# x and memory laid out by features in a one-core block kernel: loads, queues and fourteen transposes changed

## What is computed

```python
def _rmsnorm(x, g, eps=NORM_EPS):
    xf = x.astype(jnp.float32)
    y = xf * lax.rsqrt(jnp.mean(xf * xf, axis=-1, keepdims=True) + eps)
    return (y * g.astype(jnp.float32)).astype(x.dtype)
...
    x = x + 0.5 * _rmsnorm(_swiglu(_rmsnorm(x, ffn1_pre_g), ffn1_w_gu, ffn1_w_down), ffn1_post_g)
...
    kx, vx = jnp.split(_rmsnorm(mem, mem_norm_g) @ xa_w_kv, 2, axis=-1)
```

## Time and profile before

| what | value |
|---|---|
| median of 3 runs | 1097.92 us |
| the profiled execution | 1097.21 us |
| its span | 1095.4 us |
| PE busy | 1083.8 us, 99% |
| DVE busy | 797.0 us, 73% |
| ACT busy | 593.2 us, 54% |
| HBM read | 186.50 MB, 171 GB/s over the span |

### The profile page before, as it was taken

The page is one execution under the profiler, slowest core; times in us unless marked ns, Lnnn a source line. Parts: engine busy times, 40 slices in busy tenths (PEclk is TensorE's granted clock), DMA queues, the critical chain, the costliest instruction groups (busy, mean ns, idle before and its releaser), DMA issues.

```text
span 1095.4 us, 21019 instructions
## 1 busy us (share of the span) xinstructions
PE 1083.8 (99%) x8538; PEld 1029.7 (94%) x8538; DVE 797.0 (73%) x1119; ACT 593.2 (54%) x845; POOL 0.2 (0%) x4
## 2 busy tenths in 40 slices
PE   9999999999999999999999999999999998999998
PEld 7999999999999999999999988999999798999998
DVE  6665556989989867778778556765555887997774
ACT  5544445678643345878446546444444665565561
POOL 0000000000000000000000000000000000000000
PEclk9999999999999999999999999999999999999999
DMA  8765555455533354443556533465555346443341
GB/s 301 249 228 191 195 188 192 158 197 185 171 138 116 121 206 155 154 172 137 205 169 236 192 116 116 148 227 191 197 186 191 127 167 223 159 154 123 109 154 39
DMA packets 29137, 188.59 MB, mean 172 GB/s; under 512 B 3496, under 2 KB 4809, under 8 KB 7370
## 3 DMA queue, kind: packets, MB, share of 16 engines
q1 hardware_dynamic: 26592, 181.42, 47.7%
q10 hardware_dynamic: 2474, 6.15, 1.7%
HBM read 186.50 MB, written 1.05 MB: 171 GB/s over the span
## 4 chain that ended last, share of the span: by engine, by line
PE 91%; DVE 5%; ACT 2%; issue 1%; DMA 1%; SPq 0%; DVEq 0%; ACTq 0%
PE bank L520 16%; PE bank L521 16%; PE bank L522 16%; PE bank L532 11%; PE bank L533 11%; PE bank L534 11%; PE bank L619 3%; DVE sb_w_lo L2043 1%; PE bank L745 1%; PE bank L860 1%; ACT sb_w_hi L1346 1%; PE bank L1008 1%; PE bank L693 1%; PE bank L1020 1%; DMA sb_w_raw<-in_w 1%
## 5 line engine op out<-in xcount | busy, mean ns | idle before, releaser
L2043 DVE TENSOR_TENSOR sb_w_lo<-sb_w_raw,sb_w_hi 128x2048 fp32r<-128x2048 f32 x169 | 386.5, 2289 | 135.6 <-ACT sb_w_hi L1346 135.2
L1346 ACT ACTIVATE sb_w_hi<-sb_w_raw 128x2048 fp32r<-128x2048 f32 x169 | 322.9, 1911 | 34.5 <-PE bank L522 33.0
L520 PE MATMUL bank<-sb_hT_hi,sb_w_hi 128*128 128x256 f32 (+1 forms) x816 | 226.0, 277 | 0.0
L522 PE MATMUL bank<-sb_hT_hi,sb_w_lo 128*128 128x256 f32 (+1 forms) x816 | 226.0, 277 | 0.0
L521 PE MATMUL bank<-sb_hT_lo,sb_w_hi 128*128 128x256 f32 (+1 forms) x816 | 225.8, 277 | 0.0
L532 PE MATMUL bank<-sb_hT_hi,sb_w_hi 128*128 128x256 f32 (+2 forms) x744 | 212.7, 286 | 0.0
L533 PE MATMUL bank<-sb_hT_lo,sb_w_hi 128*128 128x256 f32 (+2 forms) x744 | 206.4, 277 | 0.0
L534 PE MATMUL bank<-sb_hT_hi,sb_w_lo 128*128 128x256 f32 x744 | 206.2, 277 | 0.0
L522 PEld LDWEIGHTS bank<-sb_hT_hi,sb_w_lo 128*128 128x128 f32 (+1 forms) x816 | 152.8, 187 | 0.1
L520 PEld LDWEIGHTS bank<-sb_hT_hi,sb_w_hi 128*128 128x128 f32 (+1 forms) x816 | 152.8, 187 | 0.0
L521 PEld LDWEIGHTS bank<-sb_hT_lo,sb_w_hi 128*128 128x128 f32 (+1 forms) x816 | 152.5, 187 | 0.0
(11 more groups left out here) (507 smaller groups left out, 2137.9 us busy)
## 6 DMA issues: line engine op xcount, KB each, us to landing
sb_w_raw<-in_w SPq DMA_DIRECT2D x169, 1024.0 KB, 5.0
sb_x<-in_x SPq DMA_DIRECT2D x2, 512.0 KB, 4.5
sb_w_raw<-in_w SPq DMA_DIRECT2D x4, 256.0 KB, 6.8
sb_w_raw<-in_w SPq DMA_DIRECT2D x2, 512.0 KB, 8.0
sb_mem_xn<-in_mem ACTq DMA_DIRECT2D x1, 1024.0 KB, 7.8
sb_post_g<-in_ffn_post_g ACTq DMA_DIRECT2D x2, 512.0 KB, 4.6
sb_decay<-in_c_decay ACTq DMA_DIRECT2D x1, 768.0 KB, 4.2
out<-sb_x SPq DMA_DIRECT2D x3, 256.0 KB, 2.1
```

Of the source, the lines that this page charges most:

```text
L520: pe.matmul(o, a_hi, b_hi, start=first, stop=False)
L522: return pe.matmul(o, a_lo, b_hi, start=False, stop=last)
L1346: act.activation(w_hi[b % STAGES][:], w_raw[b % RING][:], ACT.Copy).then_inc(w_hi_in, 1)
L2043: tt(w_lo[b % STAGES][:], w_raw[b % RING][:], f32(w_hi[b % STAGES][:]), ALU.subtract).then_inc(w_lo_in, 1)
```

## The change

`x` and `mem` are also handed over transposed (`xT`, `memT`). SP loads `xT` in four parts of 256 KB straight into `hT`, alternating with the four parts of block 0, and only behind block 2 the rows of `x`, the identity and `cols`. ACT's queue first loads the 8 gain columns (`first_g`); ACT and DVE multiply the even and odd feature tiles of `hT` by them in place. The transposes of `x` go. PE does one product of zeros, one that opens bank 0, and then block 0 feature tile by feature tile. The squares of `x` are both summed on ACT, behind the rounding of block 2; the root follows the remainder of block 2 on DVE; PE spreads it in the middle of up 2 (not up 1). The remainder of block 3 is written before hidden tile 0 (not behind it), and ACT rounds block 3 before it copies `rb`. Of `mem`, the root alone is spread by two transposes, in front of up 20; DVE multiplies `mem_T` by gain and root in eight pieces, ACT and DVE split it in two halves. One DVE operation of 128x2048 behind kv (`mem_T` from hi and lo, L2324) goes.

```diff
             def first_block():
-                ready = norm_done(0)
                 o = claim("up1.0", 0, 0)
+                pe.matmul(o[:], zeros[:, 0:P], zeros[:], start=True, stop=False)
                 w = w_raw[0][:].rearrange("p (k c) -> p k c", k=KD)
-                for i in range(2):
-                    for k in range(KD):
...
+                for k in range(KD):
+                    pe.wait_ge(S("x_odd" if k % 2 else "x_even"), k // 2 + 1)
...
+                    for i in range(2):
...
-                    up_block(j, between=(lambda: root_turn(n)) if j == 1 else None)
+                    up_block(j, between=(lambda: root_turn(n)) if j == 3 - n else None)
...
+                if n == 1:
+                    mem_root_turn()
                 up_block(FF_TILES - 2)
                 down_block(PAIRS - 2, 0, *LAST_DOWN[n][2])
                 up_block(FF_TILES - 1)
-
-                if n == 1:
-                    norm_turn(1, mem_xn, 1, (7, 0, 2, 1))
                 down_block(PAIRS - 1)
...
-            stay_warm(zeros[:, 0:P], zeros[:], 2)
-
-            pe.wait_ge(S("ident_in"), 16)
-            raw_turn(0, x_landed)
+            stay_warm(zeros[:, 0:P], zeros[:], 1)
...
@@ scalar
+                if n == 1:
+                    after(up_at(n, 0))
                 o = full(act, f"rb{n}")
                 copy(f"rb{n}", f["rb"][:], o[:, 0:SEQ])
                 gate(0)
...
                     act.dma_start(mem_xn[:], a["mem"].rearrange("(t p) d -> p t d", p=P)).then_inc(S("mem_in"), 16)
+                    act.dma_start(mem_T[:].rearrange("p k c -> p (k c)"), a["memT"]).then_inc(S("memT_in"), 16)
...
                 after(down_at(n, PAIRS - 2))
+                if n == 1:
+                    mem_high(0)
                 gate(FF_TILES - 1)
                 high(FF_TILES - 1)
                 after(up_at(n, FF_TILES - 1))
                 if n == 1:
-                    norm_high(1, "mem_norm_g", mem_hi)
+                    mem_high(1)
...
+            act.dma_start(first_g[:], a["cols"][:, at:at + KD]).then_inc(S("first_g_in"), 16)
+            act.wait_ge(S("zeros"), 1)
+            act.activation(ffn[1]["gate"][:, 0, :], zeros[:, 0:SEQ], ACT.Silu)
...
             round_to(STAGES)
+            for t in range(TOK):
+                act.wait_ge(S(f"x_in{t}"), 16)
+                ins = act.activation(ffn[1]["xn"][:, t, :], x[:, t, :], ACT.Square, accum_out=ssq[:, t:t + 1])
+            ins.then_inc(S("norm_ssq"), 1)
+            act.wait_ge(S("cols_in"), 16)
...
@@ vector
+                if n == 1:
+                    low_block(b)
                 wait_read(dve, f"rb{n}")
                 if n == 1:
-                    hidden_tile(0, [], [b])
+                    hidden_tile(0, [], [])
                     hidden_tile(1, [], [b + 1])
...
                     row_root(1, rstd[:, 0:2])
+                    dve.tensor_copy(mem_r[:], rstd[:, 0:2]).then_inc(S("mem_root"), 1)
...
+                    mem_normal(0, 2)
+                    hidden_tile(FF_TILES - 2, [b], [b + 1], 0, [lambda: mem_normal(2, 5), lambda: mem_normal(5, 8)])
+                    hidden_tile(FF_TILES - 1, [], [b + 2], 0, [lambda: mem_low(0)])
+                    mem_low(1)
...
+            low_to(STAGES)
             ffn_root(0)
-            low_to(STAGES)
...
@@ sync
-            for t in range(TOK):
-                sp.dma_start(x[:, t, :], a["x"][t * P:(t + 1) * P, :]).then_inc(S(f"x_in{t}"), 16)
+            n = KD // FIRST_PARTS
             for b, parts in ((0, FIRST_PARTS), (1, SECOND_PARTS), (2, 1)):
                 for part in range(parts):
+                    if b == 0:
+                        sp.dma_start(hT[:, part * n:(part + 1) * n, :].rearrange("p k c -> p (k c)"),
+                                     a["xT"][:, part * n * SEQ:(part + 1) * n * SEQ]).then_inc(S(f"xT_in{part}"), 16)
...
+            for t in range(TOK):
+                sp.dma_start(x[:, t, :], a["x"][t * P:(t + 1) * P, :]).then_inc(S(f"x_in{t}"), 16)
+            sp.dma_start(ident, a["c_square"][:, 0:P]).then_inc(S("ident_in"), 16)
+            sp.dma_start(cols[:], a["cols"]).then_inc(S("cols_in"), 16)
```

More of the change, by code:

```diff
@@ L184 @@
 SPLIT_FROM = 1
-RAW = (0, 3, 4, 5)
+RAW = (3, 4, 5)
 def columns_of(n):
     return ((0,), (1, 2), (3, 4), (5, 6), (7,)) if n in RAW else ((0, 1), (2, 3), (4, 5), (6, 7))
-COLUMNS_AT = [sum(len(columns_of(m)) for m in range(1, n)) for n in range(7)]
-BY_SCALAR, BY_VECTOR = (0, 2, 4), (1, 3)
+COLUMNS_AT = [sum(len(columns_of(m)) for m in range(2, n)) for n in range(7)]
 FOLD_AT = (0, 1, 1 + P)
@@ L338, in program @@
         mem_T = place(8, "mem_T", [P, KD, SEQ])
+        mem_r = place(80, "mem_r", [P, TOK])
+        mem_rb = place(98, "mem_rb", [P, SEQ])
         late_hi = place(32, "late_hi", [P, KD, SEQ], F32R)
@@ L1443, in ffn_part, with mem_high @@
                 rounded[0] += TURN * PAIR_TURNS
+                if n == 1:
+                    o = full(act, "mem_rb")
+                    copy("mem_rb", mem_rb[:], o[:, 0:SEQ])
+                def mem_high(side):
+                    act.wait_ge(S("mem_n"), 4 * side + 4)
+                    k = slice(4 * side, 4 * side + 4)
+                    act.activation(mem_hi[:, k, :], mem_T[:, k, :], ACT.Copy).then_inc(S("mem_hi"), 1)
                 gate(FF_TILES - 2)
@@ L1484, in out_part @@
                 after(FIRST[stage] + 3)
[L1487 to L1502, removed]
+            at = COLS["ffn1_pre_g"][0]
+            act.dma_start(first_g[:], a["cols"][:, at:at + KD]).then_inc(S("first_g_in"), 16)
+            act.wait_ge(S("zeros"), 1)
+            act.activation(ffn[1]["gate"][:, 0, :], zeros[:, 0:SEQ], ACT.Silu)
+            act.wait_ge(S("first_g_in"), 16)
+            for k in range(0, KD, 2):
+                act.wait_ge(S(f"xT_in{k // (KD // FIRST_PARTS)}"), 16)
+                act.activation(hT[:, k, :], hT[:, k, :], ACT.Copy, scale=first_g[:, k:k + 1]).then_inc(S("x_even"), 1)
+            for side in range(2):
+                act.wait_ge(S("x_even"), 2 * side + 2)
+                act.wait_ge(S("x_odd"), 2 * side + 2)
                 k = slice(4 * side, 4 * side + 4)
@@ L2219, in ffn_part, with mem_normal, mem_low @@
                 if n == 1:
[L2220 to L2223, removed]
+                    def mem_normal(first, last):
+                        for k in range(first, last):
+                            stt(mem_T[:, k, :], mem_T[:, k, :], col("mem_norm_g", k), mem_rb[:], ALU.mult, ALU.mult)\
+                                .then_inc(S("mem_n"), 1)
+                    def mem_low(side):
+                        dve.wait_ge(S("mem_hi"), side + 1)
+                        k = slice(4 * side, 4 * side + 4)
+                        tt(mem_lo[:, k, :], mem_T[:, k, :], f32(mem_hi[:, k, :]), ALU.subtract).then_inc(S("mem_lo"), 1)
+                    dve.wait_ge(S("memT_in"), 16)
+                    dve.wait_ge(S("cols_in"), 16)
+                    wait_read(dve, "mem_rb")
+                    mem_normal(0, 2)
+                    hidden_tile(FF_TILES - 2, [b], [b + 1], 0, [lambda: mem_normal(2, 5), lambda: mem_normal(5, 8)])
+                    hidden_tile(FF_TILES - 1, [], [b + 2], 0, [lambda: mem_low(0)])
+                    mem_low(1)
                 else:
@@ L2299, in _ @@
             dve.memset(zeros[:], 0.0).then_inc(S("zeros"), 1)
[L2300 to L2307, removed]
+            dve.wait_ge(S("first_g_in"), 16)
+            for k in range(1, KD, 2):
+                dve.wait_ge(S(f"xT_in{k // (KD // FIRST_PARTS)}"), 16)
+                ts(hT[:, k, :], hT[:, k, :], first_g[:, k:k + 1], None, ALU.mult).then_inc(S("x_odd"), 1)
             for side in range(2):
@@ L2992 @@
     arrays = {"x": given["x"][0], "mem": given["mem"][0]}
+    for n in ("x", "mem"):
+        arrays[n + "T"] = arrays[n].T.reshape(KD, P, SEQ).transpose(1, 0, 2).reshape(P, KD * SEQ)
     stream = np.zeros((NBLOCK, P, BLOCK), np.float32)
```

41 lines of the change are left out of this document (22 added, 19 removed).

## The result

The changed kernel takes 1104.52 us (median of 5 runs, 1102.80 to 1108.13), the kernel before 1096.92 us beside it (5 runs, 1095.55 to 1098.52): a ratio of 1.0069 with a 95% interval of 1.0046 to 1.0092. The change makes the kernel **7.6 us slower**. Forecast were 1097.4 and "same"; the range ended at 1100.0.

A forecast was written before the change was run, and what follows sets the result against it. PE, busy 99% of the span, was taken to bound the kernel. Start +1.20 and end of the first feed-forward part -1.66 gave -0.5 us: 1097.4 against the median of 1097.92, range 1094.6 to 1100.0.

The forecast's parts named there:

- The start (+1.20): Kernel start to up 6: up 1 begins 1.6 us earlier, but block 3 is rounded later; PE starts up 6 1.20 us later.
- The last link: Up 6: block 8's remainder comes 1.56 us later with 0.36 to spare, so PE starts up 6 1.20 us later.
- the rule that I had set against the sum: Loads of xT: transfers of 1 MiB or more advised for 75% of peak; quarters take 3.3 us, total 0.8 us later.
- The end of the first feed-forward part (-1.66): Before kv0: mem's transposes go, kv0 waits 0.4 us for the second half of mem_lo; 1.66 us gained.
- The sum -0.5: Whole kernel: +1.20 at the start and -1.66 at the end of the first feed-forward part give -0.5 us.
- Rivals 1, 2 and 4: 1: early start kept, 1094.6 (0.14). 2: block 3 lands late, 1100.5 (0.11). 4: mem splitting on DVE replaces transposes, 1099.1 (0.12).
- Rival 3 (0.03): Start: PE waits on first pieces, loses its 2.4 GHz clock, block 0 takes 14.3 us; +2.9 us, 1100.8; chance 0.03.

The follow-up runs named there:

- both parts: The changed kernel with first_g placed behind the placed tiles, so these stand as before the change: 1096.56 us, ratio 0.9990.
- memory alone: The kernel before with only the changed path of memory, start as before: 1095.48 us, ratio 0.9985.
- the last run: The changed kernel with first_g behind the placed tiles, and identity and cols loaded behind block 3 instead of ahead: 1097.40 us, ratio 0.9995.

## Why the prediction was wrong

**Right, in the main.** The start (+1.20): the profile of the changed kernel shows +1.23 at up 6, of which 0.22 are the slower products of down 0 and down 1, so the start costs 1.0 there. Block 3, the remainder, the tiles and down 0 follow each other as worked out, and moving 0.2 MB behind block 3 moves block 3 and down 0 together. The last link was wrong: PE didn't wait for block 8's remainder at up 6, it brought most of its delay from down 0 (+0.73, forecast +0.3) and up 3 (+1.01, forecast +0.65). That 1.23 stands so close to 1.20 is luck. In the totals it costs 2.0 (1.0 to 3.0) by itself, or 1.1 as the difference of both parts (1096.56) and memory alone (1095.48). Up 1 came at 14.04, not 13.3: block 1's first half was rounded from 11.58 and not from 10.93. It did no harm, as down 0 waits for tile 0 anyway. By the rule that I had set against the sum (the Trainium skill, DMA: Bandwidth & Descriptors, section Bandwidth) it would have come 0.8 us later than by mine, and it came 0.65 later. (The 0.8 took the rule's 75% of the peak for the quarters as well; the rule gives that share from 1 MiB up, so by it 0.8 is the least.) The stretch from 5 to 10 us moved 333 GB/s, the next 413. But the kernel before, whose x comes in bigger loads, moved 323 in the same stretch, so the trace doesn't show that the size of the pieces is the reason. The end of the first feed-forward part (-1.66): -1.6 by the trace. The sum -0.5: with the tiles back in place the full change measures -1.3 by the medians, -1.1 by the ratio (0.9990, 0.9981 to 0.9999), inside my range. Rivals 1, 2 and 4 didn't come. Rival 3 (0.03) came in part in two profiles of the changed start, for 1.0 us: I had the right mechanism, a wait on the pieces and before up 1, and took the 0.80 us gap of the earlier trace rows as a reason against it, but PE waits some 2 us before up 1. (That the zeros run at the 1.2 GHz level was read from their 0.88 us a record; the granted clock that the profile gives for that stretch is 1.00.)

**The step that failed** is one that isn't in the working. The change part by part went through the removed and the added instructions, and took every other PE step as before: behind up 6 "PE is the slower of the three and nothing more is lost", and "The 128x2048 sum of mem_T on DVE goes behind kv, beside PE's work: nothing" is its last word on the rest of the kernel. The runs show 0.9 us lost between up 6 and kv0 with PE busy throughout, and most of the rest behind it. The diff line `first_g = sb("first_g", [P, KD])` isn't costed in any sentence. It moves every placed tile by 32 bytes, and that costs 8.0 us (1104.52 against 1096.56; 7.8 by itself in the kernel before), sixteen times the sum that I had worked out. Neither a rival nor the range had anything of the kind, since every cost in them hung on a wait, a transfer or a clock. The kernel before holds a hint: it places the ffn tiles at `24 + LINE` (in KB, LINE being 64 / 1024), 64 bytes off the grid of the others, and the prediction doesn't ask what such an offset is worth.

**Open.** Why the products with hT and the weights, none of which moved, also lose 2.2 us with 32 bytes, outside the feed-forward parts, and with 64 bytes inside them too. As they read no placed tile, what the other engines do at the time with the placed tiles may have a part in it; that isn't shown. Their step goes between 113 and 118 ns from stage to stage in the kernel before too. And which two accesses get in each other's way: the runs show that the distance counts, not what is done with it inside the chip. A run that moves the weights alone wasn't made.

## What to carry to other kernels

A new tile changes the addresses of all tiles allocated behind it. When PE is 99% busy, put a small tile last, or pad it to a distance that costs nothing in your own runs (in these, 256 and 512 bytes), and compare the step of products in a stage that the change doesn't touch: if it differs, the time has moved for a reason outside the change. Run an unused tile of the same size in the old kernel as a control before a change is blamed or dropped. Here the shift hid a part worth some 1.6 us (memory's) in a result of +7.6.

## What the runs showed of the hardware

A steady stream of products of 256 columns (the 192 with `mixed`; 191 steps), by how many bytes the placed tiles stand further from the weights (and from `x`, hT_hi and hT_lo) than in the kernel before. The step is that of `mixed` alone; other operands differ, as said above.

| bytes further | stage, us | ns a step | kernel's time over before's |
|---|---|---|---|
| 0 (before) | 21.65 | 113.3 | 1 |
| 0, weights and tiles both 64 higher | 21.64 | 113.3 | 0.9998 |
| 32 (before plus an unused tile) | 22.50 | 117.8 | 1.0070 |
| 64 (changed kernel, which has its own -1.3 us) | 22.92 | 120.0 | 1.0127 |
| 128 | 22.49 | 117.8 | 1.0057 |
| 256 | 21.65 | 113.3 | 0.9987 |
| 512 | 21.65 | 113.3 | 1.0001 |

For 32 bytes the loss is the same in both kernels: 1.0070 in the one before, 1104.52 / 1096.56 = 1.0073 in the changed one.

The clock: two waits of PE, of 0.60 us in block 0 and of 2.01 before up 1, were followed by a granted clock of 0.54 over 3.5 us; with 0.23 and 1.97 it was 0.70 over the same stretch and 0.92 over the next 8 us. Waits of 1.50 and of 1.39 before up 1 alone (the changed kernel and the last run), and waits of 1.36 in block 0 and 1.52 before up 1 together (64 bytes in first_g), left it at 1.00.
